# A four-layer transformer block on one core: layer 0's q and k leave the projection with columns on partitions, and layer 3's input is transposed inside the slab in front of it

## The reference, cut to what matters

```python
# layer 0: 16 heads of 128, three groups g (dilations 1, 4, 16), w_in 2048 x 20480
h = x @ w_in
qkv = h[..., :3*3*2048].reshape(B, S, 3, 3, 16, 128);  z = h[..., 3*3*2048:]
for g in range(3):
    q = apply_rope(qkv[:, :, g, 0], cos, sin)      # x1*c - x2*s, x2*c + x1*s over the two halves of 128
    k = apply_rope(qkv[:, :, g, 1], cos, sin)
    o, l = dilated_window_attention(q, k, qkv[:, :, g, 2], window, dilation)
wts = softmax(stack(lses))
y = sum_g(wts * o) * silu(z)
x = layer_norm(ALPHA * x + y @ w_out)
# layer 2 ends: x = x + y @ w_out
# layer 3 begins: proj = rmsnorm(x, norm_g) @ w_in    # 6 x 1024 columns, and 16 for the gates a, b
```

## Time and profile before

| | |
|---|---|
| time, median of 3 runs | 2526.83 us (2523.83 to 2526.86) |
| profiled execution, own time | 2524.33 us |
| its span | 2522.6 us, 30023 instructions |
| PE / PEld busy | 2470.3 us (98%) / 2060.6 us (82%) |
| DVE / ACT / POOL busy | 1382.7 (55%) / 1233.0 (49%) / 125.0 us (5%) |
| mean DMA rate | 164 GB/s, queues 50.3% busy |
| mean granted clock of TensorE | 0.991 |

### The profile page before, as it was taken

The page is one execution under the profiler, slowest core; times in us unless marked ns, Lnnn a source line. Parts: engine busy times, 40 slices in busy tenths (PEclk is TensorE's granted clock), DMA queues, the critical chain, the costliest instruction groups (busy, mean ns, idle before and its releaser), DMA issues.

```text
span 2522.6 us, 30023 instructions
## 1 busy us (share of the span) xinstructions
PE 2470.3 (98%) x12030; PEld 2060.6 (82%) x12030; DVE 1382.7 (55%) x1848; ACT 1233.0 (49%) x1661; POOL 125.0 (5%) x125
## 2 busy tenths in 40 slices
PE   8999999999999999989999989999999999999999
PEld 6888888888888888868888868888888887888887
DVE  5645454645464646554545565555445466746554
ACT  4454444444454445344555345555444368645443
POOL 1101010101010101000000000000000000000000
PEclk9999999999999999989999989999999999999999
DMA  7545555555555554635533545555555555433344
GB/s 239 188 159 185 166 184 167 181 164 173 171 172 175 183 167 151 217 125 187 180 117 116 186 143 177 174 184 173 182 173 164 179 184 161 137 103 117 101 134 134
DMA packets 342048, 414.49 MB, mean 164 GB/s; under 512 B 19019, under 2 KB 269093, under 8 KB 341397
## 3 DMA queue, kind: packets, MB, share of 16 engines
q1 hardware_dynamic: 340500, 405.63, 50.3%
q0 software_dynamic: 1408, 6.94, 0.7%
HBM read 410.42 MB, written 2.10 MB: 164 GB/s over the span
## 4 chain that ended last, share of the span: by engine, by line
PE 92%; DVE 3%; ACT 3%; issue 1%; SPq 0%; DMA 0%; POOL 0%; DVEq 0%; ACTq 0%
PE ps L557 26%; PE ps L559 26%; PE ps L558 26%; PE ps L972 2%; PE ps L597 2%; PE ps L712 1%; DVE wlo L1659 1%; ACT whi L1099 1%; PE ps L699 1%; PE ps L773 1%; PE ps L704 1%; PE ps L772 1%; PE ps L785 0%; PE ps L696 0%; DVE x L1758 0%
## 5 line engine op out<-in xcount | busy, mean ns | idle before, releaser
L1659 DVE TENSOR_TENSOR wlo<-raw,whi 128x1024 fp32r<-128x1024 f32 (+1 forms) x774 | 950.3, 1233 | 858.0 <-ACT whi L1099 854.8
L557 PE MATMUL ps<-whi,xh 128*128 128x512 f32 (+1 forms) x3072 | 1227.4, 400 | 6.7 <-DVE wlo L1659 6.7
L559 PE MATMUL ps<-whi,xl 128*128 128x512 f32 (+1 forms) x3072 | 1198.0, 390 | 0.0
L558 PE MATMUL ps<-wlo,xh 128*128 128x512 f32 (+1 forms) x3072 | 1195.8, 389 | 0.0
L1099 ACT CAST whi<-raw 128x1024 fp32r<-128x1024 f32 (+1 forms) x774 | 801.6, 1041 | 771.3 <-PE ps L559 766.7
L557 PEld LDWEIGHTS ps<-whi,xh 128*128 128x128 f32 x3072 | 578.6, 188 | 123.0 <-issue 12.2
L559 PEld LDWEIGHTS ps<-whi,xl 128*128 128x128 f32 x3072 | 577.6, 188 | 120.4
L558 PEld LDWEIGHTS ps<-wlo,xh 128*128 128x128 f32 x3072 | 578.9, 188 | 109.7
L1177 ACT ACTIVATE work<-work,small 128x128 f32<-128x128 f32 (+1 forms) x80 | 46.1, 577 | 155.7 <-DVE small L1769 155.7
L2387 POOL TENSOR_TENSOR work<-work 128x512 f32<-128x512 f32 x48 | 77.0, 1605 | 872.4 <-DVE work L1844 488.6
L972 PEld LDWEIGHTS ps<-work 128*128 128x128 f32 x544 | 67.7, 191 | 6.1 <-DVE work L2233 2.6
(11 more groups left out here) (366 smaller groups left out, 1319.9 us busy)
## 6 DMA issues: line engine op xcount, KB each, us to landing
raw<-in_dsa_w_in SPq DMA_DIRECT2D x320, 512.0 KB, 4.5
raw<-in_ev_w_in SPq DMA_DIRECT2D x144, 512.0 KB, 4.6
raw<-in_od_w_in SPq DMA_DIRECT2D x96, 512.0 KB, 4.5
raw<-in_mla_w_in SPq DMA_DIRECT2D x48, 512.0 KB, 4.3
raw<-in_dsa_w_out SPq DMA_DIRECT2D x32, 512.0 KB, 4.6
raw<-in_mla_w_out SPq DMA_DIRECT2D x32, 512.0 KB, 4.7
raw<-in_ev_w_out SPq DMA_DIRECT2D x32, 512.0 KB, 4.6
raw<-in_od_w_out SPq DMA_DIRECT2D x32, 512.0 KB, 4.9
```

The costliest lines, as they stand in the source:

```text
L557: pe.matmul(o, xh[:, k, tokens[tb]], hi, start=start and s + l == 0, stop=False)
L558: pe.matmul(o, xh[:, k, tokens[tb]], lo, start=False, stop=False)
L559: m = pe.matmul(o, xl[:, k, tokens[tb]], hi, start=False, stop=stop and s + l == 2)
L1659: dve.tensor_tensor(whole_half(wlo[:, h % 4], n), whole_half(raw[:, h // 2 % 4, 2 * (h % 2):2 * (h % 2) + 2], n), whole_half(whi[:, h % 4] ...
```

## The change

In layer 0 a new `unit_by_blocks` replaces `unit`. A slab's two blocks of 256 columns each get a bank of their own. For q and k (`TURNED`) the 128 weight columns are the stationary operand and 256 tokens stream, so that the head dimension comes out on partitions; for v and z 128 tokens are stationary as before and the block's 256 weight columns stream. The rotation works on that form: DVE multiplies partitions 64 to 127 into 0 to 63 and the other way, POOL and DVE read tables that are turned once on PE, and DVE's sum goes to `L0.qk` directly. The 48 turns on PE with their copies on ACT are gone, and who waits for them now waits for the sums. In layer 3 `turn_x` is cut: groups 0 to 5 run behind units 0 to 2 of the last slab of layer 2, groups 6 and 7 between the two halves of `few_columns`, whose result moves to bank 4; the squares come behind it.

```diff
+            cosr, sinr = t1, t2
+            TURNED = [[n in (0, 1, 3, 4, 6, 7) for n in (2 * s, 2 * s + 1)] for s in range(5)]
...
+            def unit_by_blocks(side, k0, bank, start, stop, turned, then=None):
+                for s in range(2):
+                    h = half[0]
+                    pe.wait_ge(lo_done, h + 1)
+                    for l in range(2):
+                        k = k0 + 2 * s + l
+                        first, last = start and s + l == 0, stop and s + l == 2
+                        for b in range(2):
+                            for c in range(2):
+                                o = ps[:, bank + b, c * S:(c + 1) * S]
+                                if turned[b]:
+                                    cols = slice(b * HALF + c * P, b * HALF + (c + 1) * P)
+                                    hi, lo = whi[:, h % 4, l, cols], wlo[:, h % 4, l, cols]
+                                    pe.matmul(o, hi, xh[:, k, :], start=first and c == 0, stop=False)
+                                    pe.matmul(o, lo, xh[:, k, :], start=False, stop=False)
+                                    m = pe.matmul(o, hi, xl[:, k, :], start=False, stop=last and c == 1)
+                                else:
+                                    cols = slice(b * HALF, (b + 1) * HALF)
+                                    hi, lo = whi[:, h % 4, l, cols], wlo[:, h % 4, l, cols]
+                                    pe.matmul(o, xh[:, k, tokens[c]], hi, start=first and c == 0, stop=False)
+                                    pe.matmul(o, xh[:, k, tokens[c]], lo, start=False, stop=False)
+                                    m = pe.matmul(o, xl[:, k, tokens[c]], hi, start=False, stop=last and c == 1)
+                        if l == 1:
+                            m.then_inc(half_done, 1)
+                        else:
+                            next(side, None)
+                    half[0] += 1
+                    if s == 1 and then is not None:
+                        then()
+                    next(side, None)
...
+            def few_columns(side, n, bank, layer=None, between=None):
...
+                    if s == 0 and between is not None:
+                        between()
...
+            def turn_x(layer, groups=range(8)):
+            def turning_x(layer):
+                def then(j):
+                    return (lambda: turn_x(layer, (2 * j, 2 * j + 1))) if j < 3 else None
+                return then
...
-                    project(nothing, N, out_bank(s), fine=fine)
+                    project(nothing, N, out_bank(s), fine=fine, then=turning_x(3) if layer == 2 and s else None)
...
+                yield from turns(8)                       # PE, tables
+                pe.wait_ge(*rope_a.at(0, "raw"))
+                for n, v in enumerate((L0.cosr, L0.sinr)):
+                    for tb in range(TB):
+                        m = pe.transpose(ps[:, 6, (2 * n + tb) * P:(2 * n + tb + 1) * P], v[:, tb, 0:P], ident[:, :])
+                m.then_inc(*rope_p.up("tab"))
...
             def rope0(pair):                              # PE and ACT
-                (six turns of four transposes on PE, six copies on ACT)
+                yield from turns(7)
...
-                        pe.wait_ge(*p0_a.at(pair, "qk5"))
+                        pe.wait_ge(*p0_d.at(pair, "r5"))
...
-            turn_x(3)                                     # PE
-            few_columns(nothing, 16, 2, 3)
+            pe.wait_ge(*xt_d.at(8 * 3 + 4, "lo"))
+            few_columns(nothing, 16, Q, 3, between=lambda: turn_x(3, (6, 7)))
...
+                        act.activation(L0.cosr[:, tb, o], L0.rc[:, tb, 0:64], ACT.Sin)
+                        act.activation(L0.sinr[:, tb, o], L0.r[:, tb, 0:64], ACT.Sin, scale=1.0 if hf == 0 else -1.0)
...
+                act.wait_ge(*rope_p.at(0, "tab"))
+                act.copy(L0.cosa, ps[:, 6, 0:S])
+                act.copy(L0.sina, ps[:, 6, S:N]).then_inc(*rope_a.up("tab"))
...
-                        act.wait_ge(*p0_p.at(pair - 1, ("turn1", "turn2", "turn3", "turn5", "turn5")[s]))
+                        act.wait_ge(*p0_d.at(pair - 1, ("r1", "r2", "r3", "r5", "r5")[s]))
...
-            turn_x(3)                                     # ACT
-            side = squares(3)
-            few_columns(side)
-            run(side)
+            few_columns(nothing, lambda: turn_x(3, (6, 7)))
             act.wait_ge(half_done, half[0])
-            act.copy(L3.rdec[0:16], ps[0:16, 2, 0:S]).then_inc(*dg_a.up("rows"))
+            act.copy(L3.rdec[0:16], ps[0:16, Q, 0:S]).then_inc(*dg_a.up("rows"))
+            run(squares(3))
...
+                        else:                             # DVE, rope0, first block
+                            dve.wait_ge(*hd_p.at(2 * pair - 1, "sc"))
...
-                    dve.tensor_tensor(L0.t2[:, :, 0:64], xv[:, :, 64:P], L0.sina[:, :, 0:64], ALU.mult)
-                    dve.tensor_tensor(L0.t2[:, :, 64:P], xv[:, :, 0:64], L0.sina[:, :, 64:P], ALU.mult).then_inc(*p0_d.up(f"t{n}"))
+                    for a_, b_ in ((slice(0, 64), slice(64, P)), (slice(64, P), slice(0, 64))):
+                        m = dve.tensor_tensor(L0.t2[a_], L0.h[b_, blk], bc(L0.sina[b_], 1, 2), ALU.mult)
+                    m.then_inc(*p0_d.up(f"t{n}"))
...
-                    dve.tensor_tensor(xv, L0.t1, L0.t2, ALU.add).then_inc(*p0_d.up(f"r{n}"))
+                    dve.tensor_tensor(L0.qk[:, n], L0.t1, L0.t2, ALU.add).then_inc(*p0_d.up(f"r{n}"))
...
+                    pool.tensor_tensor(L0.t1, L0.h[:, blk], bc(L0.cosa, 1, 2), ALU.mult).then_inc(*p0_g.up(f"cos{n}"))
```

More of the change, by code:

```diff
@@ L593, in project, with project_blocks @@
                     unit(side, 4 * j, n, bank, j == 0, j == 3, fine, then and then(j))
+            def project_blocks(side, bank, turned, layer=None, then=None):
+                for j in range(4):
+                    if layer is not None:
+                        pe.wait_ge(*xt_d.at(8 * layer + 2 * j + 1, "lo"))
+                    unit_by_blocks(side, 4 * j, bank, j == 0, j == 3, turned, then and then(j))
             def four(bank, src):
@@ L598, in four @@
                 return m
-            def turn_x(layer):
-                for g in range(8):
+            def turn_x(layer, groups=range(8)):
+                for g in groups:
                     if g % 2 == 0:
@@ L731, in tensor @@
                         pe.wait_ge(*e0_a.at(pair - 1, f"out{3 + s}"))
[L732 to L733 removed]
+                    project_blocks(side, bank0(pair, s), L0.TURNED[s], 0 if pair + s == 0 else None,
+                                   then=turning_y(0, [[hd_d.at(11, "fin"), e0_a.at(7, "out3")]] + 5 * [[]]) if pair + s == 11 else None)
                 run(side)
@@ L1110, in unit, with few_columns @@
                     next(side, None)
-            def few_columns(side):
-                for _ in range(2):
+            def few_columns(side, between=None):
+                for s in range(2):
                     split(half[0] + AHEAD)
@@ L1162, in last_product @@
                 for s in range(2):
-                    project(nothing, fine)
+                    project(nothing, fine, turning_x(3) if layer == 2 and s else None)
             def layer_norm(layer):
@@ L1737, in last_product @@
                 for q in (2, 3):
-                    project(nothing, fine)
+                    project(nothing, fine, turning_x(3) if layer == 2 and q == 3 else None)
                     add(q)
@@ L2323, in delta_gates @@
                 yield
-            turn_x(3)
-            side = squares(3)
-            few_columns(side)
-            run(side)
+            few_columns(nothing, lambda: turn_x(3, (6, 7)))
+            run(squares(3))
             def gated(n):
```

55 lines of the change are left out of this document (19 added, 36 removed).

## The result

The changed kernel takes 2550.82 us (median of 4 runs, 2548.51 to 2552.19) against 2526.46 for the kernel before on the same chip: ratio 1.0098, 95% interval 1.008 to 1.0115. The profiled execution took 2550.97 us, its span 2549.2. I had forecast 2506.5, range 2494 to 2530; the time lies outside that range, and rival 1 (2555) comes closest.

A forecast was written before the change was run, and what follows sets the result against it. PE was taken to bound the kernel. Turns -21.4, projections +3.1, table transposes +0.45, Sins -1.1 and layer 3's input -1.0 gave -20.0 us: 2504.3 us profiled, 2506.5 as a median, range 2494 to 2530.

The forecast's parts named there:

- rival 1: Layer 0 projections: fixed 13 ns per matmul with 128 weight columns, step 120 ns, +51 us, median 2555 us; chance 0.15.
- What bounds: Whole kernel: PE bounds, busy all 940 us from 60 to 1000 us; other engines' work is free until PE waits.
- The shape of the projections: Layer 0 projections: 3840 matmuls of 512 columns become 7680 of 256 at 113.7 ns each, +3 us.
- Rival 2: Layer 0 projections: load and stream don't hide each other's jitter, step 116 to 117 ns, +21 to +28 us; chance 0.12.
- rival 3: Layer 0 projections: loads not hidden at this length, 225 ns a step, +858 us, 3360 in all; chance 0.01.
- The turns: Layer 0, q and k: 48 transpose groups of 0.446 us leave PE, 21.4 us off.
- DVE's rotation: Layer 0 rotation: 2.07 us a block, 0.36 more, 17 us over 48 blocks, hidden in DVE's idle time.
- The tables: Start of layer 0: eight Sins fewer on ACT shrink PE's stall, -1.1 us; four table transposes on PE, +0.45 us.
- Layer 3's entry: Layer 3's input transposes moved earlier: entry 9.8 us instead of 10.8, -1.0 us, with a 0.8 us stall remaining.

The follow-up runs named there:

- experiment 1: Kernel before, only layer 0's 512-column streams issued as two of 256, each with its own weight load: 2571.97 us against 2525.3, ratio 1.0183.
- experiment 3: Changed kernel with only 64, or 16, weight columns in each group's second and third matmul: 2527.77 us with 64, 2525.11 with 16.
- experiment 5: Changed kernel with layer 0's v and z blocks back on the old unit of 512 streamed columns: 2531.08 us, ratio 1.0019 to the kernel before.
- experiment 7: Changed kernel with hi streaming xh and xl in one 512-column matmul, v and z by the old unit: 2516.38 us against 2525.3 before, ratio 0.9962.

## Why the prediction was wrong, point by point

- **What bounds.** Right: PE is busy all of the 940 us from 60 to 1000 and has no wait from 30 to 1085 us after the change.
- **The shape of the projections.** This step failed, by the size of its one number. I took 113.7 ns, it is 120.0, and 7680 x 6.3 is 48 us, of which the times show 46.7 (experiment 1). Three rows bore on it and I weighed them wrongly: the line through the 384- and 512-column steps, matmuls of the same form with weights as wide, gave 120, but by extrapolation; the few-column rows had the right stream and the wrong weights. The place with a full load beneath (it recurs at the end of each few-column product, so it wasn't the only one) tested the load and not the matmul's own width, and experiment 3 points to the latter, by start times alone. Rival 1, a fixed part per matmul with 128 weight columns, has the cost right, 4 us off in time: 120, 173 and 227 ns lie on its line, and experiments 1, 5 and 7 came out by it within some 5 us. I gave it 0.15. Rival 2, jitter between load and stream, isn't it: over 95% of the steps between two matmuls of these blocks are 120 ns to the nanosecond. What the 13 ns are stays open.
- **The page of the Trainium skill** ("TensorE: Matmul & The Clock Gate", "LDWEIGHTS (loading the stationary operand)" and "Back-to-back issue gap") would have had 109 ns for the 256-column stream and 107 for the load. The trace has 120, and 113 for the load alone: its fixed 2.5 ns is here 13, and paid by 3840 more matmuls this difference of 10.5 ns is 40 us, more than the change loses. The sentence on loads that rival 3 cites stands in that page's section "The mechanism"; rival 3, the loads not hidden, didn't occur: its step would be 225 ns.
- **The turns.** Right in the sum: 46.7 for the split alone less 24.4 for the whole leave 22.3 us for everything else in the change; I had 21.4 + 1.1 + 1.0 - 0.45 = 23.1. No run takes the turns out alone.
- **Small slips.** 2504.3 + 2.5 is 2506.8, and a pair of heads, by -21.4 and +3.1 over eight pairs, should have taken 2.3 us less and not 2.6. Neither changes the outcome.
- **DVE's rotation.** The price of a product was right and its meeting with POOL was missed, without effect on the time. The mean of the products, 64 partitions x 512 elements, is 0.92 us, but it mixes two kinds: 73 of the 96 take 0.69, as forecast, and the 23 that run beside POOL's product take 1.67. In before 8 of the 48 first products met it so, at 1.51 against 0.42. POOL's product went from 1.6 to 1.98. So a block costs 2.5 us on average and not 2.07. With 400 us idle in 940, DVE hid it. The first two rows are groups. The others are single places: a block's two products without POOL (1.39 us), a block whose first product runs beside POOL's (2.37, that is 1.67 and 0.69), and that product of POOL.

```profile
L2435 POOL TENSOR_TENSOR work<-work 128x512 f32<-128x512 f32 x48 | 95.0, 1980 | 883.6 <-DVE work L1894 542.3 <-ACT work L1320 341.4
L1890 DVE TENSOR_TENSOR work<-work 64x512 f32<-64x512 f32 x96 | 88.6, 922 | 2.1
...
225.44 1.39 DVE L1890 TENSOR_TENSOR work<-work 64x512 f32<-64x512 f32 x2
...
238.50 2.37 DVE L1890 TENSOR_TENSOR work<-work 64x512 f32<-64x512 f32 x2
...
237.48 2.15 POOL L2435 TENSOR_TENSOR work<-work 128x512 f32<-128x512 f32 x1 [3.37 <-DVE work L1894]
```

- **The tables.** Right on ACT, half right on PE. There are 16 Sins, and the next cast of ACT comes at 37.11, 2.15 us behind the first Sin against 3.31. The stall of 1.28 us is gone, but not only for that: the Sins themselves begin 1.3 us later than before, and the cast comes no sooner (it was at 36.94). The kernel of experiment 1 has all 24 Sins and the 120 ns steps, and there the stall is 0.69 us. So some 0.6 of the 1.28 us went because PE, with its longer steps, came later, which I had not reckoned with, and 0.7 is what the missing Sins can be credited with. The first two rows are of after, the third is of experiment 1.

```profile
34.96 0.26 ACT L1273 ACTIVATE work<-work 128x64 f32<-128x64 f32 x1 [4.32 <-DVE work L1873]
...
37.11 3.97 ACT L1139 CAST whi<-raw 128x1024 fp32r<-128x1024 f32 x4
```
```profile
40.65 0.38 PE L560 MATMUL ps<-whi,xh 128*128 128x256 f32 x1 [0.69 <-DVE wlo L1673]
```

- **Layer 3's entry.** Right: 1.3 us gained, 1.0 forecast. The two late groups show as gaps of 0.16 and 0.08 us over the regular step (2054.65 to 2054.93, 2055.51 to 2055.71), 0.25 us where I had 0.8, since the casts ran faster than their means (ACT's four in 1.57 us, DVE's in 1.66). The squares didn't hold up PE.

## What to carry to other kernels

When a change alters the shape of the instructions on the bounding engine, the pace of the new shape is the prediction: take it from rows that agree in every size the new one has (columns streamed *and* columns of weights), and where none does, prefer the line through rows of the same form over a row that differs in kind. A product in few-column weights is no stand-in for a full one. On an engine without gaps, count instructions as well as columns: here, at full clock, a matmul with its load costs its columns and some 13 ns, so halving streams costs and joining two streams over one set of weights (experiment 7) gains. And a mean over a group can mix two kinds of instruction; before reading it as a price, look at single ones.

## What the runs showed of the hardware

- In this reduced fp32 format a matmul with 128 weight columns and a load of its own recurs every 120.0, 173 and 227 ns at 256, 384 and 512 streamed columns, at full clock: columns / 2.4 and 13 ns. The 256-column step is strikingly regular.
- At half clock the 13 ns aren't there. In the first slab of the changed kernel 22 steps of 256 columns take 4.69 us, 213 ns each, which is 256 / 1.2, at a granted clock of 0.50. The 512-column step of before at half clock is 428 ns (2160.95 to 2163.09, five steps), so by these rows halving a stream would cost nothing there; no run tried it.

```profile
17.30 0.41 PE L587 MATMUL ps<-xh,wlo 128*128 128x256 f32 x1
...
21.99 0.41 PE L588 MATMUL ps<-xl,whi 128*128 128x256 f32 x1
```
```profile
16.00:22.00 6.00, 5.05 (x24) 5.08 (x25) 4.75 (x4) 2.49 (x3) 4.23 (x5) 0.50 1.10 348
```

- With fewer columns of weights a 256-column stream recurs sooner, but by no simple rule: every 113 ns with 64 (layer 1) and 116 to 118 with 64 in experiment 3; 113 with 16 over a full load there, and 117 with 16 in layer 3 of the changed kernel; 117 with 8 in layer 2.
- With shorter streams the loads bind, at 113 ns each over a group of three (112 with one streamed column and fp32 operands).
- A DVE product of two fp32 inputs over 64 partitions x 512 elements took 0.69 us alone, as long as the sum over 128 partitions, and 1.67 us where POOL's product of two inputs ran beside it.
